# Adding the squares of two chunks in f32 before the multiplication by ones, in three norms of an eight-core decoder layer

## The reference, cut to what matters

```python
def _rmsnorm(x, g):
    x32 = x.astype(jnp.float32)
    y = x32 * lax.rsqrt(jnp.mean(x32 * x32, axis=-1, keepdims=True) + EPS)
    return (y * g.astype(jnp.float32)).astype(x.dtype)

def _swiglu(x, wg, wu, wd):
    return (jax.nn.silu(x @ wg) * (x @ wu)) @ wd

# _mla: q = _rmsnorm(cq, q_norm) @ w_uq      cq (B,S,384)
#       kv = _rmsnorm(ckv, kv_norm) @ w_ukv   ckv (B,S,256)

def reference(...):
    h = x
    h = h + 0.5 * _swiglu(_rmsnorm(h, ffn1_norm), ffn1_wg, ffn1_wu, ffn1_wd)
    h = h + _mixer(h, mem, positions, mix_norm, ...)   # latent attention, gated linear
                                                       # attention and cross-attention, merged
    h = h + 0.5 * _swiglu(_rmsnorm(h, ffn2_norm), ffn2_wg, ffn2_wu, ffn2_wd)
    return _rmsnorm(h, final_norm)
```

## Time and profile before

| | |
|---|---|
| median of 3 runs | 1683.11 us (lowest 1680.85) |
| the profiled execution's own time | 1687.72 us |
| span of its slowest core (core 1) | 1686.6 us; the eight cores: 1673.0 to 1686.6 us |
| PE busy | 1628.0 us, 97% of the span, 7859 matmuls |
| DVE busy | 872.0 us, 52%, 1490 instructions |
| ACT busy | 730.4 us, 43%, 1182 instructions |
| POOL busy | 120.6 us, 7% |
| mean granted TensorE clock | 0.992 to 0.995 on the eight cores |

### The profile page before, as it was taken

One profiled execution on the slowest core, in us unless ns is written; L12 is line 12 of the kernel. 1 busy time (PEld: TensorE's weight loads), 2 busy tenths in 40 slices (PEclk: granted clock), 3 DMA queues, 4 the chain that ended last, 5 costly groups with the idle time before them and its releaser, 6 DMA issues.

```text
span 1686.6 us, 24322 instructions; the slowest of 8 cores (1673.0 to 1686.6 us)
## 1 busy us (share of the span) xinstructions
PE 1628.0 (97%) x7859; PEld 753.9 (45%) x7859; DVE 872.0 (52%) x1490; ACT 730.4 (43%) x1182; POOL 120.6 (7%) x228
## 2 busy tenths in 40 slices
PE   6999999998999999999999999999999999999997
PEld 2445444434444444444444444454444444444443
DVE  6662442435765566654565644645645464433336
ACT  5213001046872256952477862268993221210114
POOL 0102011100000000000000000000000011001000
PEclk9999999999999999999999999999999999999999
DMA  9779999898566575555998774886464455623212
GB/s 212 106 114 124 139 125 110 129 148 208 104 146 157 151 154 111 111 130 167 252 207 181 159 192 151 256 220 154 133 192 129 159 157 157 178 70 100 76 38 100
DMA packets 80425, 249.10 MB, mean 148 GB/s; under 512 B 9440, under 2 KB 13808, under 8 KB 79856
## 3 DMA queue, kind: packets, MB, share of 16 engines
q0 software_dynamic: 28864, 107.49, 38.2%
q1 hardware_dynamic: 51440, 140.06, 26.9%
HBM read 282.91 MB, written 54.00 MB: 200 GB/s over the span
## 4 chain that ended last, share of the span: by engine, by line
PE 89%; DMA 4%; DVE 3%; ACT 3%; issue 2%; POOL 0%; DVEq 0%; ACTq 0%; SPq 0%; POOLq 0%
PE ps_all L562 88%; DMA ring<-f1g 2%; ACT mb L588 1%; DVE hS L600 1%; DMA ring<-wb 1%; ACT ma L588 1%; ACT L588 1%; DMA ring<-f2d 1%; DVE ntm L600 0%; DMA hS<-x 0%; DVE mb L595 0%; ACT fa L588 0%; DVE aF L595 0%; DVE gU L600 0%; ACT B L611 0%
## 5 line engine op out<-in xcount | busy, mean ns | idle before, releaser
L562 PE MATMUL ps_all<-ntm,ring 128*128 128x512 bf16 x2224 | 530.5, 381 | 5.1 <-ACT ma L588 2.2
L562 PE MATMUL ps_all<-B,ring 128*128 128x512 bf16 x2016 | 450.4, 379 | 2.8 <-DVE gU L600 1.0
L562 PEld LDWEIGHTS ps_all<-ntm,ring 128*128 128x128 bf16 x2224 | 216.3, 98 | 267.1 <-issue 21.1
L588 ACT ACTIVATE fa<-ps_all 128x512 f32<-128x512 f32 x170 | 101.4, 598 | 468.9 <-PE ps_all L562 460.5
L562 PEld LDWEIGHTS ps_all<-B,ring 128*128 128x128 bf16 x2016 | 195.9, 98 | 237.7 <-issue 8.3
L562 PE MATMUL ps_all<-aF,ring 128*128 128x512 bf16 (+1 forms) x1264 | 294.3, 375 | 3.7 <-DVE hS L600 1.7
L600 DVE SCALAR_TENSOR_TENSOR hS<-ps_all,hS 128x512 f32<-128x512 f32 (+1 forms) x256 | 170.0, 672 | 99.6 <-PE ps_all L562 98.4
L595 DVE TENSOR_TENSOR aF<-fa,ps_all 128x512 bf16<-128x512 f32 x148 | 101.3, 686 | 226.0 <-PE ps_all L562 219.6
L562 PEld LDWEIGHTS ps_all<-aF,ring 128*128 128x128 bf16 x1264 | 123.4, 98 | 147.5 <-issue 10.7
L588 ACT ACTIVATE mb<-ps_all 128x512 bf16<-128x512 f32 (+1 forms) x304 | 161.5, 576 | 39.0 <-PE ps_all L562 36.0
L588 ACT ACTIVATE ma<-ps_all,hv 128x512 f32<-128x512 f32 x104 | 71.2, 687 | 183.1 <-PE ps_all L562 162.2
(11 more groups left out here) (129 smaller groups left out, 1215.1 us busy)
## 6 DMA issues: line engine op xcount, KB each, us to landing
ring<-wb SPq DMA_DIRECT2D x112, 512.0 KB, 4.4
ring<-f1g POOLq DMA_DIRECT2D x44, 512.0 KB, 10.4
ring<-f2bg POOLq DMA_DIRECT2D x44, 512.0 KB, 3.6
wb<-wm POOLq DMA_DIRECT2D x28, 512.0 KB, 14.7
ma<-spill SPq DMA_DIRECT2D x48, 256.0 KB, 5.5
ring<-wb SPq DMA_DIRECT2D x48, 256.0 KB, 3.7
ring<-f2g POOLq DMA_DIRECT2D x22, 512.0 KB, 8.6
f2bg<-ring SPq DMA_DIRECT2D x22, 512.0 KB, 5.5
```

The lines of the kernel that those rows point to most:

```text
L562: i = e.matmul(_ap(o), lhsT=_ap(l), rhs=_ap(r), start=st, stop=sp)
L588: f.add([("act", lambda e: e.activation(out=_ap(out), in_=_ap(in_), func=func, scale=_ap(scale), **kw), c_act(out, bias is not None))], ou ...
```

## The change

`take` with a bank kind now squares two chunks into f32 tiles of M2, DVE adds them into a bf16 tile, and one ones matmul follows for the two: 4 instead of 8 per tile. `self.p` is opened at the second chunk instead of the first. `mean_square` does the same for pairs where the bank kind is "m"; the third chunk of the 384 norm stays single. In all: three closings in `ffn1a` and one in `ffn2b` (4 x 4 = 16 ones matmuls fewer, 16 DVE additions more), and four mixer tiles (each 5 to 3 ones matmuls and 2 additions: 8 fewer, 8 more). The tail `ending`, the norms of the opening and the memory norm stay as they are.

```diff
-    def mean_square(srcs, dim, n, banks, narrow):
+    def mean_square(srcs, dim, n, banks, wide, narrow):
         p = bank(banks)
-        for i, s in enumerate(srcs):
+        pairs = [srcs[i:i + 2] for i in range(0, len(srcs), 2)] if banks in ('m',) else [[s_] for s_ in srcs]
+        for i, two in enumerate(pairs):
             sq = narrow.get()
-            actf(sq[:, 0:n], s, AF.Square, scale=dim ** -0.5)
-            mm([(p[:, 0:n], ones, sq[:, 0:n], i == 0, i == len(srcs) - 1)])
+            if len(two) == 2:
+                w = [wide.get(), wide.get()]
+                for v, s in zip(w, two):
+                    actf(v[:, 0:n], s, AF.Square, scale=dim ** -0.5)
+                tt(sq[:, 0:n], w[0][:, 0:n], w[1][:, 0:n], ALU.add)
+                wide.put(*w)
+            else:
+                actf(sq[:, 0:n], two[0], AF.Square, scale=dim ** -0.5)
+            mm([(p[:, 0:n], ones, sq[:, 0:n], i == 0, i == len(pairs) - 1)])
             narrow.put(sq)
         return p
...
         def take(self, src):
+            self.n += 1
+            if self.kind is not None:
+                if self.n % 2:
+                    self.half = self.wide.get()
+                    actf(self.half, src, AF.Square, scale=D ** -0.5)
+                    return
+                sq = self.wide.get()
+                actf(sq, src, AF.Square, scale=D ** -0.5)
+                both = self.narrow.get()
+                tt(both, self.half, sq, ALU.add)
+                self.wide.put(self.half, sq)
+                if self.n == 2:
+                    self.p = bank(self.kind)
+                mm([(self.p, ones, both, self.n == 2, self.n == 8)])
+                self.narrow.put(both)
+                return
             sq = self.narrow.get()
             actf(sq, src, AF.Square, scale=D ** -0.5)
-            self.n += 1
-            if self.kind is not None:
-                if self.n == 1:
-                    self.p = bank(self.kind)
-                mm([(self.p, ones, sq, self.n == 1, self.n == 8)])
-                self.narrow.put(sq)
-                return
```

More of the change, by code:

```diff
@@ L726, in rmsnorm @@
         wide, narrow = wide or M2, narrow or M1
-        p = mean_square(srcs, dim, n, banks, narrow)
+        p = mean_square(srcs, dim, n, banks, wide, narrow)
         rstd = wide.get()
```

## The result

The changed kernel takes 1709.58 us (median of 7 runs, lowest 1706.95), the kernel before 1681.70 in the same comparison: a ratio of 1.0163 [1.0151, 1.0175], **27 us slower**. I had forecast 1688 and a range of 1677 to 1698. The result lies outside the range, though still within 2% of the kernel before.

What follows compares the result with a forecast made beforehand. PE was taken to bound the kernel, with DVE pacing the closings. +6.9 (`ffn1a`) + 0 (`ffn2b`) - 1.7 (mixers) = +5.2 us on a median of 1683.1 gave 1688 us, range 1677 to 1698.

Steps and rivals of the forecast that it cites:

- What bounds the kernel: Whole kernel: PE bounds it, busy 1628.0 of 1686.6 us; in the closings DVE goes from well below PE to above it.
- Removed and added: Closings and mixers: 24 ones matmuls go, 5.2 us of PE; 24 DVE additions of 0.691 us come, 16.6 us.
- The first wait of a closing: Each of four closings: PE's gap before the first ones matmul grows from 1.67 to 2.6 us, +0.9 each.
- The walk through `ffn1a`: Close of `ffn1a`, PE and DVE order carried forward: first projection at about 402 instead of 395.14, +6.9 us.
- the second load: Close of `ffn1a`: tile 3's second load, issued at 379.10, can't go earlier, so tile 2's third chunk starts at about 388.5.
- `ffn2b` zero: Closing of `ffn2b`: +0.9 us for the longer wait, -0.9 for 4 saved ones matmuls, zero in sum.
- The mixers -1.7: Low-rank norms of four mixer tiles: 5 ones matmuls become 3, -0.43 us each, -1.7 in all.
- The clock zero, 3 in the bound: Longer gaps in the `ffn1a` close may bring one or two more half-speed dips: 0 in the sum, 3 us in the upper bound.
- rival B: Mixers: new order makes PE's 20.6 us of short waits grow by half, +10 us, 1698; chance 0.17, downward 0.03.
- The sign that I had set for it: Mixers: PE's idle time moving by more than 5 us either way would show the new order outweighing the closing.

Runs made afterwards that it cites:

- pinned order: Engine, stream place and bank of each operation taken over from the kernel before; with all pairs 1691.69 us (1.0039), with pairs in the closings only 1691.87 us (1.0039).
- Three orders that contain nothing of the change: Kernel before without pairs: planner's DVE constant 0.137 instead of 0.135 (1.0102), 0.133 (1.0084), or the f32 pool of wide tiles turned (1.0077).
- pairs in the order of before: All pairs of the change, with engine, place and bank of each operation taken from the kernel before's list: 1691.69 us, 1.0039.
- its eight neighbours: Newly planned orders, against the kernel before: 0.133, 0.137 or turned pools without pairs; pairs in norms or `ffn1a` only; changed kernel at 0.133, 0.135, 0.137: 1.0056 to 1.0163.

## Why the prediction was wrong

By its own steps.

- **What bounds the kernel.** Right: PE, and DVE in the close of `ffn1a`.
- **Removed and added.** Right: 24 ones matmuls and 24 additions, these at 690 ns, the f32 squares at 629, as taken from the earlier trace rows. The 9 casts that moved to DVE were not foreseen, they are the planner's doing.
- **The first wait of a closing**: expected 2.6, measured 2.85 in `ffn1a`, 2.84 and 2.85 in `ffn2b`. The two updates and the two squares ran back to back, and the addition could start only at 360.12. That the wait had been 1.67 in all four closings was a misreading: for tile 0 it was 0.32. Nothing hung on it, since the walk goes by the spacing of the tiles.
- **The walk through `ffn1a`.** Tile 1's first ones at 360.96 (360.9 expected); the three ones of tile 0's turn done by 372.24 (372.5); tile 0's behind tile 1's by 11.3 us (11.6); tile 2's third chunk at 386.14 (388.5). There the second load was misjudged: SP issued all four loads in one go from 375.88, instead of half of them at 379.10. The projection followed at 399.92, +4.8 by its time and +5.1 from the start of the closing, where I had +6.9. By the mean over the eight cores it is +6.9. Right in the mechanism and, on a typical core, in size, with some luck in the second: the walk came to 45.3 us from the start of the closing, where the cores took 44.2, and started from core 1 with its 38.6, where the cores of before took 37.3.
- **`ffn2b` zero**: slightly too small (the run with pairs there alone: +2.2 us [0.5, 3.9]).
- **The mixers -1.7**: not seen, and not refuted. In a pinned order the runs with and without the norms' pairs differ by nothing, but a difference of 1.7 us would be lost in their intervals.
- **The clock zero, 3 in the bound.** Too small. The dip after 372.46 lay in the closing and was foreseen as possible; but the new waits in the mixers brought dips of their own, as from 652 to 664 us. By windows of 42 us the clock's part grew by 10.4 us.
- **The step that failed** is the one that I left at zero in the sum and priced as rival B: "the new order costs in the mixers". I took the short waits there (20.6 us) as a quantity that could grow or shrink by half with chances of 0.17 and 0.03, and zero as the likeliest. Measured from the first projection to the end it is +16.6 us (+17.0 as a mean over the cores), with at most 12 removed matmuls (2.6 us) against it. Three orders that contain nothing of the change lose 13 to 17 us in all, 9 to 15 of them in this part. The sign that I had set for it, PE's idle time in the mixers moving by more than 5 us, was just not reached (20.6 to 25.1): the loss also came as a lower clock and as 4.0 us of idle time from 1265 on, which that sign did not look at. So zero was the wrong centre: I knew that all streams behind 357 us were new, and that in the kernel before PE was idle for 0.1 us in the 377 us from 1261 on the earlier trace rows. In a stretch like that another order has no wait to remove and can only add some; the mixers, with a fortieth of idle time, are not far from it. The centre of that term belonged on the side of a loss. At the +10 of rival B the forecast would have been 1698, and with the +13 to +17 of the runs 1701 to 1705.
- **What the sum came to.** The parts that the runs can price: pairs in the order of before +6.6 us (1.0039), a new order without pairs +13 to +17 (1.0077 to 1.0102). Together +20 to +24 of the 27 us. By the cut at the first projection it is +7 in the close (+3.8 in the order of before), and +17 behind it, at the upper end of what the draws gave (-1.5 to +17). How much of those 17 the pairs behind the projection add is not separated by any run; with pairs in `ffn1a` alone it is +14.5 without them.
- **Still open.** Why the planner's order of before is better than seven of its eight neighbours: all orders but the pinned ones follow from the same rules, and I have only seen that different waits turn up (the rope-key copies, weights by DMA, normed chunks ahead of `aF`), not that one rule makes them. Nor was it tried whether a bank of its own for the sums, outside the line of kind "f", would free the closings.

## What to carry to other kernels

When a planner makes the order, split a change into what it computes and the order that it draws: measure it in the order of before, and draw a few other orders without it (here a cost moved by 2 ns moved the kernel by 1%). Where the bounding engine is full for hundreds of microseconds, centre the forecast of a new order on a loss: seven of eight were one here. And cut the traces of all cores at the same event, not only those of the slowest. In the closings a saved matmul of 0.22 us did not pay for the addition of 0.69 us and the wait for a second chunk that came with it; that it would pay where both lie under other work of PE is likely, but no run here shows it.

## What the runs showed of the hardware

- A wait of 1.67 us was followed by full clock at 359 us in the kernel before, and one of the same length at 1641 us by a clock of 0.73 in the stretch from 1640 to 1644, so the length of a wait did not decide it. In the changed kernel one of 1.74 us at 372 us, the last of four in 12 us, was followed by a clock of 0.67 and 0.76 in the next two stretches of 3 us, and one of 2.60 us at 652 by 12 us at 0.50 to 0.61. I had counted waits and not what came behind them. The rows of the changed kernel by stretch, behind 372 us:

```profile
372.00:375.00 3.00, 2.76 (x9) 1.11 (x10) 0.10 (x1) 0.00 (x0) 0.00 (x0) 0.67 1.07 305
375.00:378.00 3.00, 3.00 (x12) 1.17 (x11) 1.74 (x3) 1.06 (x2) 0.00 (x0) 0.76 0.98 335
```

- The page "TensorE: Matmul & The Clock Gate" of the Trainium skill says in "A second HAM failure mode: psum-queue depth-cycling" that short idles between groups of matmuls can make the clock go up and down. The closings of the changed kernel agree with it (four waits of 0.46 to 2.85 us in 12 us, and then 0.67), more than I had given it.
- A tensor-tensor operation on two f32 tiles of 128x512 on DVE took 690 ns with a bf16 result (the 56 additions of the changed kernel) and 692 with an f32 one (`ma<-ma`, 32 of them), and a square on ACT 628 ns with a bf16 result and 629 with an f32 one: the type of the result made no difference in either.
